# A two-layer decoder trunk on one core: first stage and turn of layers reordered, squares of x moved from GpSimd to ScalarE

## The chip, the core and the metric

The kernel runs on one core of a Trainium2 chip. The metric is the device time of one execution in microseconds (us). Of the kernel before three runs are shown, with a median of 2258.12 us (2257.59 to 2258.47); one more execution was taken with the profiler. Engines are TensorE (PE; its weight loads PEld), VectorE (DVE), ScalarE (ACT), GpSimd (POOL) and SyncE (SP), which here only issues loads and stores.

## The reference

One sequence of 256 tokens with 2048 features passes two layers (DEPTH is 2), all in float32:

```python
for i in range(DEPTH):
    u = rms_norm(h, norm_mix_g[i]) @ w_in[i]
    y_pool = multiscale_pool(u[..., :o1], pool_w[i], pool_scale[i])
    y_att = latent_attention(u[..., o1:o2], u[..., o2:o3], u[..., o3:], cos, sin, ...)
    h = h + jnp.concatenate([y_pool, y_att], axis=-1) @ w_out[i]
    h = h + conv_gated_ffn(rms_norm(h, norm_ffn_g[i]), w_up[i], conv_w[i], conv_b[i], w_down[i])
    gate = jax.nn.sigmoid(rms_norm(h, norm_ple_g[i]) @ w_ple_gate[i])
    h = h + (p[i] @ w_ple[i]) * gate
return rms_norm(h, final_norm_g)
```

rms_norm divides each token's features by the root of their mean square and multiplies by a gain. The inner width of the FFN is 5632, the latents have 512 features each, and cos and sin are rotary tables from the positions.

## The kernel before

**Arithmetic.** Each product of float32 matrices is made of three matmuls on a split (`three`, L1417 to L1421): both operands are cut in a rounded part `hi` and a rest `lo`, and hi x hi, lo x hi and hi x lo are added in PSUM. So each weight passes ScalarE (a copy to `w_hi`, L618 or L837) and VectorE (`w_lo = raw - w_hi`, L1016) ahead of TensorE.

**Weights.** All weights stream in chunks of 1 MB (2048 columns by 128 partitions) through four slots of `raw`, issued by SyncE (`load`, L347). A chunk is split in two halves of 1024 columns, into six slots of `w_hi` and `w_lo`. ScalarE and VectorE work AHEAD = 4 halves ahead: `steps(l, a, b)` makes the splits of halves a+4 to b+3. The semaphores that order this are raw_landed, hi_done, lo_done and w_used.

**Activations.** h holds the residual, tokens on partitions. `turn_h` transposes 256 of its columns on TensorE (four transposes, L1476) into one bank of PSUM; `gained` copies the bank to `hi` on ScalarE with the norm's gain as scale (L637) and the rest to `lo` on VectorE (L1027). One such piece is a "job"; the eight jobs of the first norm are `mix_job(l, 0..7)`. The norm's per-token factor comes later: it is applied when the product is read from PSUM (`latent`, L685), so the mean square is needed only there. GpSimd turns sums of squares into that factor (`factor`).

**First stage.** SyncE issues the rows of the gains (four loads), the conv taps and bias (three loads), and then the chunks of w_in. ScalarE issues the positions and blocks 0 and 1 of x, GpSimd blocks 2 and 3 (a block is 512 columns of h, 512 KB). TensorE transposes the rows of the gains, which VectorE copies to `prm` (L1003) once its 18 set-up steps of the rotary angles (L965 to L999) are done; then it makes turns 0 to 3, transposes taps and bias (L1492), and enters the loop over layers. The first product (block "cq") has eight halves; turns 4, 5 and 6, 7 follow its second and fourth half. ScalarE takes sine and cosine (L628, L629, each function with its table load), jobs 0 and 1, splits 0 and 1, jobs 2 and 3, and in the loop splits 2 to 5, jobs 4 and 5, the squares of block 3 of x, splits 6 and 7, jobs 6 and 7. GpSimd builds the bands of the pooling, and then squares blocks 0 to 2 of x (`sq_x`, L523) and adds them up in nine halving steps (L528).

**Turn of the layers.** In the last stage of a layer (the gate of the per-layer input, four blocks) each block of h becomes final in `gate(j)` on VectorE. ScalarE squares blocks 0 to 2 between the splits there, and block 3 in the next layer, or behind the loop after the last. The halves of the last block are followed by turns 0 to 3 of the next layer, jobs 0 to 3, splits 0 and 1 of the next layer, and then `gate_tanh(3)` and `gate(3)`. These run in the last layer too, where nothing uses them. At the end GpSimd makes the last factor, VectorE scales h (L1402), and SyncE stores it.

Of the kernel before, what the change touches and what calls it, by code (L numbers as in the profile page):

```python
# [114 lines left out]
def build(nc, x, p, positions, norm_mix_g, w_in, pool_w, pool_scale, q_norm_g, w_uq, kv_norm_g, w_ukv,  # L115
# [37 lines left out]
    with ExitStack() as ctx:  # L153
# [3 lines left out]
        def sem(name):  # L157
            return ctx.enter_context(nc.semaphore(name))


        raw = sb("raw", [P, RAW_SLOTS, CHUNK])
# [11 lines left out]
        band_lo = sb("band_lo", [P, len(POOL_WINDOWS), 16], F32R)  # L173
# [5 lines left out]
        krt = (sb("krt_hi", [P, 2, S], F32R), sb("krt_lo", [P, 2, S], F32R))  # L179
        sumsq = sb("sumsq", [P, TT, N_BLK])  # L180
        sumsq_lat = sb("sumsq_lat", [P, 2, TT])
        rstd = {n: sb(f"rstd_{n}", [P, TT]) for n in ("mix", "q", "kv", "ffn", "ple", "final")}
# [4 lines left out]
        mx = sb("mx", [P, 2, TT])  # L187
        nmx = sb("nmx", [P, 2, TT])
        psums = sb("psums", [P, 2, TT])
        prec = sb("prec", [P, 2, TT])  # L190


        with ExitStack() as scope:
# [11 lines left out]
            sq_x = sb("sq_x", [P, TT, N_BLK - 1, BLK], scope=scope)  # L205
# [38 lines left out]
        raw_landed = [sem(f"raw_landed{i}") for i in range(RAW_SLOTS)]  # L244
        slot_seen = sem("slot_seen")
# [22 lines left out]
        x_sq = sem("x_sq")  # L268
# [37 lines left out]
        HJ = KT // 2  # L306

# [28 lines left out]
        def _(sp):  # L336
# [30 lines left out]
            sp.dma_start(rows_g[POOL_S:POOL_S + PKT], pool_scale.rearrange("l (k p) -> k l p", p=P)).then_inc(  # L367
                rows_landed, 16)


# [6 lines left out]
            with sp.Fori(0, L) as l:  # L377
                c = CH["cq"]
                for k in range(KT // 4):
                    load(l, c, square(w_in, l, k, D_POOL))  # L380
                    c += 1
# [65 lines left out]

            for c in range(AHEAD // 2):
# [11 lines left out]
        def _(pool):  # L460
# [23 lines left out]
            for j in range(2, N_BLK):  # L484
                load_x(pool, j)
# [1374 lines left out]
```

## Time and profile before

| | us |
|---|---|
| median of three runs | 2258.12 |
| the profiled execution | 2256.0 |
| its span, first to last instruction | 2254.4 |
| TensorE busy | 2217.3 (98%) |
| VectorE busy | 1387.4 (62%) |
| ScalarE busy | 1046.5 (46%) |
| GpSimd busy | 66.5 (3%) |

The profiled execution is 1.6 us longer than its span and 2.1 us below the median. "Busy" is the time in which an engine has an instruction under way; matmuls overlap, so one of 0.39 us may follow the one before by less. The granted clock is TensorE's, as a share of full speed. An entry such as "PE acc L1419 <- DVE w_lo L1016: 6.1, 2, 5.1" reads: TensorE waited for VectorE's w_lo, 6.1 us in total, 2 times, at most 5.1 us.

### The profile page before, as it was taken

The page shows a single profiled execution, that of the slowest core. Times are in us where ns is not written, and L with a number is a line of the kernel's source. Part 1 is how long each engine was busy: PE and PEld are TensorE (multiplying, and loading weights), DVE is VectorE, ACT ScalarE, POOL GpSimd, SP SyncE. Part 2 cuts the span into 40 slices and gives each one's busy share as a digit, 9 for nine tenths or more (in the row PEclk, how much of TensorE's full clock was granted, in tenths as well). Part 3 has the DMA queues.
Part 4 walks back from the last instruction along what each step waited for, and adds up shares of the span by engine and source line. Part 5 has one row for each costly group of instructions (what it writes and reads, how often), then busy time and mean ns, then how long its engine had stood idle before and what let it go on. Part 6 is the DMA issues. An engine that isn't in the chain of part 4 may idle for free.

```text
span 2254.4 us, 31518 instructions
## 1 busy us (share of the span) xinstructions
PE 2217.3 (98%) x10594; PEld 1856.8 (82%) x10594; DVE 1387.4 (62%) x1768; ACT 1046.5 (46%) x1353; POOL 66.5 (3%) x152
## 2 busy tenths in 40 slices
PE   6999999999999999999999999999999999999997
PEld 5898888888888888888888988888888888888885
DVE  6567566565666565666466665566656566666755
ACT  4545544444444444446454554444444444444553
POOL 7000000000000000000000000000000000000000
PEclk9999999999999999999999999999999999999998
DMA  6653555556555555555556355555555655555562
GB/s 202 206 167 130 203 177 186 186 177 196 186 186 186 186 174 199 186 172 196 173 179 186 132 169 187 180 197 176 190 179 171 201 198 175 189 180 170 188 217 75
DMA packets 233597, 406.60 MB, mean 180 GB/s; under 512 B 14937, under 2 KB 50217, under 8 KB 233385
## 3 DMA queue, kind: packets, MB, share of 16 engines
q1 hardware_dynamic: 232041, 401.87, 53.8%
q0 software_dynamic: 656, 2.63, 0.3%
q10 hardware_dynamic: 816, 1.05, 0.2%
q8 instruction: 44, 0.72, 0.1%
q14 instruction: 40, 0.33, 0.0%
HBM read 403.42 MB, written 2.10 MB: 180 GB/s over the span
## 4 chain that ended last, share of the span: by engine, by line
PE 97%; DVE 1%; issue 1%; DMA 0%; ACT 0%; SPq 0%; DVEq 0%; ACTq 0%; POOLq 0%; POOL 0%
PE acc L1419 31%; PE acc L1421 31%; PE acc L1420 31%; PE tps L1476 3%; PE tps L1420 0%; PE tps L1421 0%; DMA raw<-in_w_in 0%; PE tps L1419 0%; DVE w_lo L1016 0%; PE tps L1669 0%; DVE h L1402 0%; ACT w_hi L618 0%; DVE xa_lo L1027 0%; DVE sg L1369 0%; DVE h L1374 0%
## 5 line engine op out<-in xcount | busy, mean ns | idle before, releaser
L1016 DVE TENSOR_TENSOR w_lo<-raw,w_hi 128x1024 fp32r<-128x1024 f32 (+1 forms) x770 | 919.2, 1224 | 506.8 <-ACT w_hi L837 355.2
L837 ACT ACTIVATE w_hi<-raw 128x1024 fp32r<-128x1024 f32 x508 | 525.9, 1059 | 512.2 <-PE acc L1421 512.2
L1419 PE MATMUL acc<-w_hi,xa_hi 128*128 128x512 f32 (+1 forms) x1792 | 690.5, 385 | 10.9 <-DVE w_lo L1016 6.1
L1421 PE MATMUL acc<-w_lo,xa_hi 128*128 128x512 f32 (+1 forms) x1792 | 687.1, 383 | 0.0
L1420 PE MATMUL acc<-w_hi,xa_lo 128*128 128x512 f32 (+1 forms) x1792 | 686.7, 383 | 0.0
L1419 PEld LDWEIGHTS acc<-w_hi,xa_hi 128*128 128x128 f32 x1792 | 337.5, 188 | 75.8 <-issue 10.4
L1421 PEld LDWEIGHTS acc<-w_lo,xa_hi 128*128 128x128 f32 x1792 | 337.1, 188 | 65.5
L1420 PEld LDWEIGHTS acc<-w_hi,xa_lo 128*128 128x128 f32 x1792 | 337.5, 188 | 64.2
L618 ACT ACTIVATE w_hi<-raw 128x1024 fp32r<-128x1024 f32 (+1 forms) x262 | 263.9, 1043 | 159.7 <-PE acc L1421 150.3
L1419 PE MATMUL acc<-w_hi,gt_hi 128*128 128x512 f32 x640 | 254.7, 398 | 0.0
L1420 PE MATMUL acc<-w_hi,gt_lo 128*128 128x512 f32 x640 | 253.1, 395 | 0.0
L1421 PE MATMUL acc<-w_lo,gt_hi 128*128 128x512 f32 x640 | 253.1, 395 | 0.0
L1419 PE MATMUL acc<-w_hi,xb_hi 128*128 128x512 f32 x560 | 220.7, 394 | 0.0
L1421 PE MATMUL acc<-w_lo,xb_hi 128*128 128x512 f32 x560 | 218.2, 390 | 0.0
L1420 PE MATMUL acc<-w_hi,xb_lo 128*128 128x512 f32 x560 | 218.1, 389 | 0.0
L1234 DVE TENSOR_TENSOR h<-acc,h 128x512 f32<-128x512 f32 x192 | 123.3, 684 | 89.9 <-PE acc L1421 89.9
L1421 PEld LDWEIGHTS acc<-w_lo,gt_hi 128*128 128x128 f32 x640 | 120.3, 188 | 28.9
L1420 PEld LDWEIGHTS acc<-w_hi,gt_lo 128*128 128x128 f32 x640 | 120.4, 188 | 28.0
L1419 PEld LDWEIGHTS acc<-w_hi,gt_hi 128*128 128x128 f32 x640 | 120.4, 188 | 27.9
L1421 PEld LDWEIGHTS acc<-w_lo,xb_hi 128*128 128x128 f32 x560 | 105.1, 188 | 22.2
L1419 PEld LDWEIGHTS acc<-w_hi,xb_hi 128*128 128x128 f32 x560 | 105.2, 188 | 21.3 <-DVE w_lo L1016 0.4
L1420 PEld LDWEIGHTS acc<-w_hi,xb_lo 128*128 128x128 f32 x560 | 105.2, 188 | 20.9
(204 smaller groups left out, 1365.4 us busy)
## 6 DMA issues: line engine op xcount, KB each, us to landing
raw<-in_w_up SPq DMA_DIRECT2D x176, 1024.0 KB, 5.1
raw<-in_w_down SPq DMA_DIRECT2D x88, 1024.0 KB, 5.0
raw<-in_w_out SPq DMA_DIRECT2D x32, 1024.0 KB, 5.1
raw<-in_w_ple_gate SPq DMA_DIRECT2D x32, 1024.0 KB, 5.1
raw<-in_w_in SPq DMA_DIRECT2D x24, 1024.0 KB, 5.4
raw<-in_w_ukv SPq DMA_DIRECT2D x8, 1024.0 KB, 5.8
raw<-in_w_in SPq DMA_DIRECT2D x8, 864.0 KB, 4.8
raw<-in_w_uq SPq DMA_DIRECT2D x6, 1024.0 KB, 5.9
```

The costliest lines, as they stand in the source:

```text
L618: copy(w_hi[:, half_of(m), 0:n], raw[:, c % RAW_SLOTS, at:at + n], ACT.Copy).then_inc(hi_done, 1)
L837: copy(w_hi[:, half_of(m), :], raw[:, c % RAW_SLOTS, (m % 2) * HALF:(m % 2 + 1) * HALF], ACT.Copy).then_inc(hi_done, 1)
L1016: dve.tensor_tensor(w_lo[:, half_of(m), 0:n], raw[:, c % RAW_SLOTS, at:at + n], w_hi[:, half_of(m), 0:n].bitcast(F32), ALU.subtract).then_ ...
L1234: dve.tensor_tensor(hb, acc[b % 2][:, t, :], hb, ALU.add).then_inc(acc_free[b % 2], 1)
L1419: pe.matmul(dst, a_hi, b_hi, start=first, stop=False)
L1420: pe.matmul(dst, a_lo, b_hi, start=False, stop=False)
L1421: return pe.matmul(dst, a_hi, b_lo, start=False, stop=last)
L1476: ins = pe.transpose(bank[:, i * S + t * P:i * S + (t + 1) * P], tiles(t, i), ident[:, :])
```

## The change

- Loads: the first chunk of w of each layer is loaded in two transfers of half the size, the first with a semaphore of its own (`load_first`). ScalarE's queue issues block 0 of x, then the gains' rows, then blocks 1 to 3 of x. SyncE's queue issues the positions, taps and bias, then w. GpSimd's queue has no x.
- Squares: `sq_x` and its sums are gone from GpSimd. ScalarE squares all four blocks of x in the first stage, and of h in the same place of the next layer, or all four behind the loop after the last layer.
- Order: four halves instead of two are split before the loop and before each turn of layers (split 0 ahead of jobs 0 and 1, split 1 behind them, splits 2 and 3 behind jobs 2 and 3); sine, cosine and their table loads move between split 1 and job 2. VectorE copies the first gains in the middle of the angle steps. Taps and bias are transposed between turns 1 and 2. TensorE waits for one job per half instead of for two jobs per two halves.
- Buffers: small tiles are merged or declared first, so that the large buffers start at multiples of 512 bytes.

```diff
+            def load_first(l):
+                sp.wait_ge(lo_done, 2 * CHUNKS * l + 2)
+                sp.sem_inc(slot_seen, 1)
+                for i, landed in enumerate((first_landed, raw_landed[0])):
+                    sp.dma_start(raw[:, 0, i * HALF:(i + 1) * HALF].rearrange("p (a b) -> p a b", b=BLK),
+                                 rows(w_in, l, 2 * i, 2, D_POOL, BLK)).then_inc(landed, 16)
...
-            for i, g in enumerate((norm_mix_g, norm_ffn_g, norm_ple_g)):
-                sp.dma_start(rows_g[KT * i:KT * (i + 1)], g.rearrange("l (k p) -> k l p", p=P)).then_inc(
-                    rows_landed, 16)
...
+                sp.dma_start(pos_i[:, :], positions.rearrange("o (t p) -> p (o t)", p=P)).then_inc(pos_landed, 16)
...
-            for j in range(2, N_BLK):
-                load_x(pool, j)
...
-            for j in range(N_BLK - 1):
-                pool.wait_ge(x_landed[j], 16)
-                hb = h[:, :, j * BLK:(j + 1) * BLK]
-                pool.tensor_tensor(sq_x[:, :, j, :], hb, hb, ALU.mult).then_inc(x_sq, 1)
-            steps, width = N_BLK - 1, BLK // 2
-            while width:
...
             load_x(act, 0)
-            load_x(act, 1)
+            for i, g in enumerate((norm_mix_g, norm_ffn_g, norm_ple_g)):
+                act.dma_start(rows_g[KT * i:KT * (i + 1)], g.rearrange("l (k p) -> k l p", p=P)).then_inc(
+                    rows_landed, 16)
+            act.dma_start(rows_g[POOL_S:POOL_S + PKT], pool_scale.rearrange("l (k p) -> k l p", p=P)).then_inc(
+                rows_landed, 16)
+            for j in range(1, N_BLK):
+                load_x(act, j)
...
+            split(0, 0)
             act.wait_ge(prm_ready, 1)
             mix_job(0, 0)
             mix_job(0, 1)
-            split(0, 0)
             split(0, 1)
+            act.wait_ge(dve_setup, DVE_REDUCED)
+            copy(sin[:, :, :], red[:, 0], ACT.Sin).then_inc(act_setup, 1)
+            copy(cos[:, :, :], red[:, 1], ACT.Sin).then_inc(act_setup, 1)
+            copy(table_word[:, :], inv_freq[:, 0:1], ACT.Tanh)
             mix_job(0, 2)
             mix_job(0, 3)
+            split(0, 2)
+            split(0, 3)
...
+                def x_squares(j):
+                    act.wait_ge(x_landed[j], 16)
+                    squares(l, j, j - N_BLK + 1)
+                steps(l, 0, 2)
                 for i in range(4, 6):
                     mix_job(l, i)
-                squares(l, N_BLK - 1, 0)
+                x_squares(0)
                 steps(l, 2, 4)
                 for i in range(6, 8):
                     mix_job(l, i)
-                steps(l, 4, 8)
+                x_squares(1)
+                steps(l, 4, 5)
+                x_squares(2)
+                steps(l, 5, 6)
+                x_squares(3)
+                steps(l, 6, 8)
...
-                squares(l, 2, 2 * N_BLK + 3)
+                steps(l, e0 + 30, e0 + 34)
                 act.wait_ge(prm_ready, l + 3)
                 for i in range(4):
                     mix_job(l + 1, i)
-                steps(l, e0 + 32, e0 + 34)
+                steps(l, e0 + 34, e0 + 36)
                 gate_tanh(3)
-            squares(L, N_BLK - 1, 0)
+            for j in range(N_BLK):
+                squares(L, j, j - N_BLK + 1)
...
+            def first_gains():
+                dve.wait_ge(prm_t, 1)
+                dve.tensor_copy(prm[:, 0:ROWS_G], acc[1][:, 0, 0:ROWS_G]).then_inc(prm_ready, 1)
...
+            first_gains()
             magic = 1.5 * 2.0 ** 23
...
-                    jobs_split(l, JB["mix"] + 2 * i + 1)
-                    square_halves(l, m, b, xa, 2 * i, 2 * i + 2)
+                    for k in (2 * i, 2 * i + 1):
+                        jobs_split(l, JB["mix"] + k)
+                        square_halves(l, m, b, xa, k, k + 1)
```

## Rows read from the trace of the kernel before

**Rows 1.** Page: busy time and instructions; the costliest line (count, busy us, mean ns).
```profile
PE 2217.3 (98%) x10594; PEld 1856.8 (82%) x10594; DVE 1387.4 (62%) x1768; ACT 1046.5 (46%) x1353; POOL 66.5 (3%) x152
...
L1016 DVE TENSOR_TENSOR w_lo<-raw,w_hi 128x1024 fp32r<-128x1024 f32 (+1 forms) x770 | 919.2, 1224 | 506.8 <-ACT w_hi L837 355.2
```

**Rows 2.** TensorE's waits, whole run: total us, times, longest us.
```profile
PE acc L1419 <- DVE w_lo L1016: 6.1, 2, 5.1
PE acc L1419 <- DVE xa_lo L1027: 4.7, 1, 4.7
PE tps L1476 <- ACT up_tok L856: 2.9, 2, 1.4
```

**Rows 3.** Windows: us, busy of PE, PEld, DVE, ACT, POOL, clock, DMA share, GB/s.
```profile
3.00:7.00 4.00, 0.00 (x0) 0.00 (x0) 3.56 (x15) 0.82 (x1) 4.00 (x21) 1.00 0.96 243
...
17.40:20.20 2.80, 2.75 (x7) 2.17 (x8) 2.80 (x5) 0.97 (x3) 2.73 (x5) 1.00 1.05 387
...
36.50:40.70 4.20, 4.20 (x10) 3.33 (x11) 4.20 (x6) 0.00 (x0) 3.93 (x4) 0.50 0.39 132
```

**Rows 4.** Timeline to the first matmul: start us, us, engine, operation [idle before].
```profile
4.30 53.32 SPq L347 DMA_DIRECT2D raw<-in_w_in  x12
...
14.92 2.00 ACT L618 ACTIVATE w_hi<-raw 128x1024 fp32r<-128x1024 f32 x2 [3.41 <-DMA raw<-in_w_in]
...
17.45 0.79 PE L1419 MATMUL acc<-w_hi,xa_hi 128*128 128x512 f32 x1 [5.12 <-DVE w_lo L1016]
```

**Rows 5.** VectorE in the first stage; then ns (shortest/median/longest) of L1016 and L523.
```profile
22.82 11.97 DVE L1016 TENSOR_TENSOR w_lo<-raw,w_hi 128x1024 fp32r<-128x1024 f32 x4 [1.28 <-ACT w_hi L618]
...
L1016 DVE TENSOR_TENSOR w_lo<-raw,w_hi x2: 2911/2912/2914, 24.7 to 27.5; 128x1024 fp32r<-128x1024 f32 x2
...
L523 POOL TENSOR_TENSOR sq_x<-h x3: 1893/2869/2876, 21.8 to 26.4; 128x1024 f32<-128x1024 f32 x3
```

**Rows 6.** ScalarE's table load; ScalarE's queue, 3 to 7 us; x's landing; angle steps.
```profile
8.55 1.28 ACT L631 ACT_TABLE_LOAD   x1
9.85 0.20 ACT L631 ACTIVATE table_word<-inv_freq 128x1 f32<-128x1 f32 x1
...
q10 hardware_dynamic: 483, 0.95, 93.5%
...
DMA to landing us min/median/max: 4.7/7.1/8.7
...
4.41 0.23 DVE L984 TENSOR_SCALAR turns<-turns 128x128 f32<-128x128 f32 x1
...
6.57 1.53 DVE L999 TENSOR_SCALAR red<-red 128x128 f32<-128x128 f32 x1
```

**Rows 7.** Timeline: the factor's end, normalised rows on VectorE; TensorE's turns of them (chain).
```profile
44.92 0.73 POOL L547 TENSOR_TENSOR rstd_mix<-mean,consts 128x2 f32<-128x2 f32 x1
...
54.19 0.88 DVE L1071 TENSOR_SCALAR lat<-lat,rstd_q 128x512 f32<-128x512 f32 x2
...
59.15 0.95 PE tps L1476 x8
```

**Rows 8.** Timeline at the turn of the layers: ScalarE and TensorE.
```profile
1135.74 3.90 ACT L618 ACTIVATE w_hi<-raw 128x1024 fp32r<-128x1024 f32 x4 [2.63 <-issue]
...
1139.14 0.50 PE L1419 MATMUL acc<-w_hi,xa_hi 128*128 128x512 f32 x1 [1.01 <-DVE w_lo L1016]
```

**Rows 9.** Chain of the last matmuls (first and last of 13); timeline of the last squares.
```profile
2235.92 0.23 PE acc L1421
...
2238.64 0.24 PE acc L1421
...
2242.73 0.63 ACT L657 ACTIVATE sq_h<-h 128x512 bf16<-128x512 f32 x1 [2.56 <-DVE h L1374]
```

**Rows 10.** TensorE's lines by form: count, busy us, mean ns, idle before.
```profile
L1420 PE MATMUL acc<-w_hi,xa_lo 128*128 128x512 f32 x1664 | 649.0, 390 | 0.0
...
L1420 PE MATMUL acc<-w_hi,gt_lo 128*128 128x512 f32 x640 | 253.1, 395 | 0.0
```

More of the change, by code:

```diff
@@ L158, in sem @@
             return ctx.enter_context(nc.semaphore(name))
+        sumsq = sb("sumsq", [P, TT, N_BLK])
+        sumsq_lat = sb("sumsq_lat", [P, 2, TT])
+        rstds = sb("rstds", [P, 6, TT])
+        rstd = {n: rstds[:, i, :] for i, n in enumerate(("mix", "q", "kv", "ffn", "ple", "final"))}
+        band_lo = sb("band_lo", [P, len(POOL_WINDOWS), 16], F32R)
         raw = sb("raw", [P, RAW_SLOTS, CHUNK])
@@ L186, in build @@
         C_D, C_LORA, C_EPS, C_POWER, C_HALF = range(5)
[L187 to L190, printed above, removed]
+        soft = sb("soft", [P, 4, 2, TT])
+        mx, nmx, psums, prec = (soft[:, i] for i in range(4))
         with ExitStack() as scope:
@@ L378, in _ @@
                 c = CH["cq"]
-                for k in range(KT // 4):
-                    load(l, c, square(w_in, l, k, D_POOL))
-                    c += 1
+                load_first(l)
+                for k in range(1, KT // 4):
+                    load(l, c + k, square(w_in, l, k, D_POOL))
+                c += KT // 4
                 for col in (D_POOL + LORA, D_POOL + LORA + LW):
@@ L928, in _ @@
                 gate_tanh(0)
[L929 to L931 removed]
+                steps(l, e0 + 12, e0 + 20)
                 gate_tanh(1)
                 pw_out(1)
[L934 removed]
                 steps(l, e0 + 20, e0 + 30)
                 gate_tanh(2)
[L937 to L938 removed]
+                steps(l, e0 + 30, e0 + 34)
                 act.wait_ge(prm_ready, l + 3)
@@ L1037, in mix_job @@
                 gained(l, JB["mix"] + i, xa, 2 * i, G_MIX + 2 * i, hT_hi, 3 * HJ * l + i + 1)
+            split(0, 0)
             mix_job(0, 0)
             mix_job(0, 1)
-            split(0, 0)
             split(0, 1)
@@ L1044, in _ @@
             mix_job(0, 3)
+            split(0, 2)
+            split(0, 3)
             dve.wait_ge(prm_t, 2)
@@ L1059, in _ @@
                 dve.wait_ge(prm_ready, l + 2)
-                steps(l, -2, 2)
+                steps(l, 0, 2)
                 for i in range(4, 6):
@@ L1382, in _ @@
                 gate(2)
-                steps(l, e0 + 30, e0 + 32)
+                steps(l, e0 + 30, e0 + 34)
                 dve.tensor_copy(prm, prm_all[:, bass.ds(l + 1, 1), :].rearrange("p a b -> p (a b)")).then_inc(
@@ L1391, in _ @@
                     mix_job(l + 1, i)
-                steps(l, e0 + 32, e0 + 34)
+                steps(l, e0 + 34, e0 + 36)
                 gate(3)
@@ L1487, in _ @@
                 turn_h(0, JB["mix"], i)
-            pe.wait_ge(conv_landed, 16 * 3)
-            pe.wait_ge(prm_ready, 1)
-            for l in range(L):
-                pe.transpose(acc[1][:, l, TAP[0]:TAP[2]], rows_c[0][:, l, :], ident[0:2 * FKT, 0:2 * FKT])
-                ins = pe.transpose(acc[1][:, l, TAP[2]:G_Q], rows_c[1][:, l, :], ident[0:2 * FKT, 0:2 * FKT])
-            ins.then_inc(prm_t, 1)
+                if i == 1:
+                    pe.wait_ge(conv_landed, 16 * 3)
+                    pe.wait_ge(prm_ready, 1)
+                    for l in range(L):
+                        pe.transpose(acc[1][:, l, TAP[0]:TAP[2]], rows_c[0][:, l, :], ident[0:2 * FKT, 0:2 * FKT])
+                        ins = pe.transpose(acc[1][:, l, TAP[2]:G_Q], rows_c[1][:, l, :],
+                                           ident[0:2 * FKT, 0:2 * FKT])
+                    ins.then_inc(prm_t, 1)
             with pe.Fori(0, L) as l:
```

56 lines of the change are left out of this document (17 added, 39 removed).

## The prediction

> **What bounds the kernel now.** I read the busy times first. TensorE is busy 2217.3 of 2254.4 us, so neither a faster copy nor a faster load in the middle of a layer can show; only TensorE's 37 us of idleness and its slow stretches can [rows 1]. The view of waits, taken for TensorE alone, says where it stands inside the run: 5.1 us for the first split of w, 4.7 us for a split of x, 1.0 us for another split of w, and twice 1.4 us for up_tok, which the change does not touch [rows 2]. To this come the start before any operand has landed and 15.5 us of tail (2254.4 less 2238.88, the end of the last matmul) [rows 9]. So the case is decided in the first 50 us, at the turn of the layers, and in the tail.
>
> The windows of the first stage then show a second loss. From 36.5 to 40.7 us, right behind the wait of 4.7 us, the granted clock is 0.50 (1.2 GHz): 10 matmuls took 4.2 us [rows 3]. At full clock one follows the other by 0.227 us (2238.64 less 2235.92, over 12, in the chain of waits) [rows 9]; 10 of them are 2.3 us, so the slow clock costs 1.9 us. The first matmuls run at the low pace too: 7 in the 2.75 us from 17.45, where 12 would have fitted [rows 3, 4].
>
> **The squares of x leave GpSimd: the largest term.** Behind the wait of 4.7 us stands VectorE: four subtractions of w_lo took 11.97 us in the very stretch in which GpSimd squares x [rows 5]. Two of them lasted 2.91 us each and GpSimd's squares 2.87 us; the mean of all 770 is 1.22 us [rows 1, 5]. VectorE is held while GpSimd works on x. The Trainium skill (SBUF — State Buffer, "SBUF: two separate sides") says that the pair of ports which these two engines share is an exclusive lock, taken also by a VectorE operation with two SBUF inputs against a GpSimd operation that reads SBUF. By that rule, the trace agrees: durations equal in pairs.
>
> With the squares on ScalarE these subtractions cost 1.23 us. The four give back 7 us of VectorE time and the wait of 4.75 us (31.74 to 36.49) goes whole, with its slow clock of 1.9 us: together **6.7 us**. What is late next? I laid out the eight halves of the first block with 1.05 us per copy of w, 0.78 us per pair of gained copies, 1.23 us per subtraction, 0.83 us per pair of gained subtractions, 1.27 us per block of squares. TensorE needs 12 x 0.227 = 2.72 us a half and 1.05 us for each group of eight turns. ScalarE does 8 copies, 4 pairs and 4 squares from the loop's head, 16.6 us in the 25 us that TensorE takes. With the start below (first matmul at 14.7) the third half is ready 2.3 us ahead of TensorE, the fifth 2.0 us, the seventh 2.5 us: no stall. The fifth is the tightest because ScalarE waits there for VectorE's copies of the gains (1.3 us), which follow the fourth half.
>
> The skill's price for a table switch speaks against this. The trace first: a load took 1.28 us, and the next activation began 0.02 us after it [rows 6]. Two such loads and three small activations, 3.3 us, now stand on ScalarE between the second split and the third x job. The skill (ScalarE: Activation LUTs, "What ACT_TABLE_LOAD costs") gives about 2.66 us a switch, with a drain. By that figure ScalarE would be 2.8 us later, and the third and fifth halves would stall 0.9 us in all. I go by the row.
>
> The mean square is later, relative to the block: the fourth square ends as TensorE finishes the block, and GpSimd's factor takes some 2.2 us more, five small operations of which the last is 0.73 us [rows 7]. So ScalarE reads the block 0 to 1.5 us later than the 0.3 us of before. The cover is there: the normalised rows were ready at 55.07 and TensorE turned them at 59.15, 4.1 us of slack [rows 7]. Cost 0.
>
> **The start.** Before, the 1 MB chunk was issued at 4.30 and landed by 14.92, and the first matmul came at 17.45 [rows 4]. Three things decide now.
> - Loads. While x was on ScalarE's queue it had 93.5% of the busy time, with rows waiting on SP's, at 243 GB/s; later w alone ran at 387 GB/s [rows 3, 6]. [...] The first block of x landed 4.7 us after issue, the median block 7.1 [rows 6]; issued at 0.93 it lands at 5.6. Behind it come 0.24 MB of small rows (0.8 us) and half a chunk (0.52 MB at 387: 1.35 us). With a transfer ending some 1.1 us ahead of its landing, the half lands at about 8. The second block had landed by 9.7 at the latest (8.07, when TensorE's turns began, and two groups of 0.8 us each); with the rows and one or two halves between, 2.2 to 3.5 us, less 0.5 for the earlier issue, it comes at 10 to 12.5. If instead all of x goes first (2.1 MB at 243 are 8.6 us) the half lands at 14.
> - VectorE. The copy of the first gains moves ahead of the last eight steps of the angles, and these ran 4.41 to 8.10, 3.7 us [rows 6]. They now wait for the gains' rows, which lie behind x's first block: landed at about 8, transposed and copied 0.7 us later at 8.75, steps until 12.4 (11.2 if the last, 1.53 us beside GpSimd's memset, is short). Then split 1.35 us, x job 0.83 us, 0.15 us to TensorE: first matmul at **14.7**.
> - Issues. ScalarE's queue now issues four loads of x and four of rows, 0.5 and 0.4 us each: until 4.6, then its first table load of 1.28, before anything has landed. Positions stay first, on SP's queue, which carries the taps next. GpSimd is rid of two issues, and its bands are done sooner. The taps' transposes move between the second and third turn and wait for gains (8.75) and taps, under VectorE's steps.
> - TensorE. Its own order asks for the second block of x and eight turns (1.7 us) before the loop: 11.7 to 14.2. Hidden.
>
> That is 2.75 us gained. Bounds: 13.0 (VectorE's steps short, gains early) and 17.5 (all x first), a gain of 0 to 4.5 us. I take 2.75, from the row of VectorE's steps, which hold even if the load is 2 us late. The six slow matmuls at the start remain. The block ends at 14.7 + 21.8 + 1.2 + 2.1 = 39.8 us against 49.5.
>
> **The turn of the layers.** Behind its last gate_tanh ScalarE lost 2.63 us, with nothing that it waited for, before it began the next layer's splits at 1135.74, and TensorE stood 1.01 us before 1139.14 for them [rows 8]. Now these two halves are split ahead of gate_tanh and the loop's edge, behind the first two, in what was ScalarE's idle time before the first turns of the new layer (that is the move of steps e0+32 to e0+34). Fifth and sixth halves, needed 5 us later, cover the edge. The squares of three blocks leave the layer's end and join the next layer's first 24 us. **1.0 us** gained; at least 0, at most 1.0.
>
> **The tail.** After the last matmul: gate_tanh, gate, squares of block 3, three operations on GpSimd, eight on VectorE. All four squares now come after gate_tanh. ScalarE idled 2.56 us before 2242.73 [rows 9], so it is free at 2240.17; four blocks of 2 x 0.63 us end at 2245.3, where one ended at 2244.1. Loss **1.3 us** (rounded up by GpSimd's steps). If leaving the loop costs ScalarE what its repetition did (2.63 us), it is 3.8 us. I take 1.3: the program runs on straight there.
>
> **Nothing.** One more issue of some 0.4 us per layer for the half loads: at the second layer no wait for a landing is among TensorE's [rows 2]. The merged tiles and the new semaphores put no instruction on TensorE's path. The 512-byte starts: TensorE's pace shows no mark of where its operands lie, 0.390 and 0.395 us for the second product with xa_lo and gt_lo, which lie in different buffers [rows 10]. From 1 ns lost to 1 ns won on 8,688 such matmuls would be 9 us either way, so this zero is the widest of the bounds; I keep it as a rival.
>
> **Sum.** -2.75 - 6.65 - 1.0 + 1.3 = -9.1 us. The profiled execution took 2256.0 us (1.6 around the span of 2254.4), now 2246.9; the median of 2258.12 goes to **2249.0**.
>
> **Rivals.**
> - *All x first.* x on one queue keeps the SP queue out, as between 3 and 7 us. First matmul at 17.5, gain 6.35: 2251.8. Against: that share was measured with two transfers of x and only tiny ones beside them.
> - *ScalarE becomes the bound.* Two table loads, four squares and a fixed order: if the fifth half is late by 5 us, TensorE stalls 3 and pays 1.9 for the clock: 2253.9. For: only 2.0 us of slack, on steps estimated one by one. Against: the rest of the first stage has 2 us to spare at each half.
> - *GpSimd was not the cause.* If the subtractions stay at 2.9 us, the 6.65 us stay: 2255.6. Against it the pairs of equal durations.
> - *Slower: the addresses.* All large buffers move by some hundred bytes. Place: each matmul that reads them. Price: 1 ns each is 8.7 us, and from 1.05 ns on (9.1 over 8,688) the kernel is not faster; at 2 ns it takes 2266. For it speaks only that the same matmul's second product has 0.390 and 0.395.
> - *The tail's edge*: 3.8 for 1.3: 2251.5.
>
> **Chances.** Forecast 0.62 (its own range 2246 to 2251), all x first 0.13, tail's edge 0.08, ScalarE 0.07, GpSimd not the cause 0.05, addresses 0.05, a third of that a gain. This kernel can be told from no change at 0.2%, 4.5 us: below 2253.6 is faster. The first three are, with a third of ScalarE's case and the addresses' gain: 0.87. Within 0.2%: 0.10, the rest of ScalarE's case and GpSimd's. Slower: 0.03, the addresses. Range 2245.0 to 2253.8: below, the earliest start (1.75 more) and a tail that costs nothing; above, ScalarE's case.
>
> **What would show it.** Right: w_lo at 1.2 to 1.4 us throughout the first 40 us; no wait over 2 us on TensorE after its first matmul; clock 1.00 from 20 us on; ScalarE's reading of the first block at about 40; no wait at 1130 us; squares from 2240.2 to 2245.3 and an end 15 to 17 us after the last matmul. Wrong: a first matmul after 16, w's first half behind all of x; a wait for ScalarE before the third or fifth half; a first square later than 2241; a pace other than 0.227 us.

## The result, and the profile after

The changed kernel takes **2231.93 us** (median of 4 runs, 2231.72 to 2233.44); the kernel before took 2257.86 us beside it (median of 4, 2256.82 to 2258.47). The ratio is 0.9887, with a 95% interval of 0.987 to 0.9904: 25.9 us faster, where 9.1 were forecast, and below the range of the prediction. The profiled execution took 2233.44 us around a span of 2231.8, so the two profiled spans differ by 22.6 us. The medians differ by 3.3 us more, because the profiled execution of before lies 1.9 us under its median and that of after 1.5 us above. The sums below are made on the spans.

Busy times and TensorE's waits of the changed kernel (TensorE's lines stand eight lines lower in the code: L1419 to L1421 are now L1427 to L1429; the subtraction of w_lo, L1016, is L1023):

```profile
PE 2203.0 (99%) x10594; PEld 1855.2 (83%) x10594; DVE 1383.2 (62%) x1770; ACT 1053.6 (47%) x1368; POOL 47.3 (2%) x138
...
L1023 DVE TENSOR_TENSOR w_lo<-raw,w_hi 128x1024 fp32r<-128x1024 f32 (+1 forms) x772 | 914.5, 1214 | 506.8 <-ACT w_hi L844 352.1
```

```profile
PE acc L1422 <- DMA rows_g<-in_pool_scale: 6.7, 1, 6.7
PE tps L1484 <- ACT up_tok L863: 2.9, 2, 1.4
PE tps L1484 <- DMA h<-in_x: 2.0, 1, 2.0
PE acc L1427 <- DVE xa_lo L1034: 0.8, 1, 0.8
```

Of the waits of [rows 2], the 6.1 us for w_lo are gone (5.1 at the start, 1.0 at the turn of the layers) and the 4.7 us for xa_lo in the first stage as well; what is left of them is 2.8 us ahead of the first matmul. But look at the first line against [rows 1]: TensorE executes the same 10594 instructions and is busy **14.3 us less**. A kernel that only lost waits would be busy as long as before. The slow clock of [rows 3] did not return, which is 1.9 us of it; against that, 12 matmuls instead of 6 run at the low pace at the start (below), about 1.2 us more. The rest needs another source.

Timeline of the start (start us, us, engine, operation, idle before), then of the rest of the first block:

```profile
3.12 1.02 SPq L353 DMA_DIRECT2D raw<-in_w_in  x2
...
7.22 0.22 DVE L978 COPY prm_all<-acc 128x56 f32<-128x56 f32 x1 [0.55 <-PE acc L1422]
...
9.78 0.24 DVE L1008 TENSOR_SCALAR red<-red 128x128 f32<-128x128 f32 x1
...
10.98 1.06 ACT L615 ACTIVATE w_hi<-raw 128x1024 fp32r<-128x1024 f32 x1 [4.28 <-DMA raw<-in_w_in]
...
11.59 1.97 PE L1484 MATMUL tps<-ident,h 128*128 128x128 f32 x8 [1.99 <-DMA h<-in_x]
...
12.13 1.23 DVE L1023 TENSOR_TENSOR w_lo<-raw,w_hi 128x1024 fp32r<-128x1024 f32 x1 [2.10 <-ACT w_hi L615]
...
14.37 0.79 PE L1427 MATMUL acc<-w_hi,xa_hi 128*128 128x512 f32 x1 [0.81 <-DVE xa_lo L1034]
```

```profile
25.12 2.36 DVE L1023 TENSOR_TENSOR w_lo<-raw,w_hi 128x1024 fp32r<-128x1024 f32 x2 [1.29 <-ACT w_hi L615]
...
39.40 1.43 POOL L536 TENSOR_TENSOR rstds<-mean,consts 128x2 f32<-128x2 f32 x1
...
40.53 0.29 PE L1427 MATMUL acc<-w_hi,xa_hi 128*128 128x288 f32 x1
...
40.86 1.27 ACT L692 ACTIVATE lat<-acc,rstds 128x512 f32<-128x512 f32 x2 [1.87 <-POOL rstds L536]
```

The first matmul comes at 14.37 us (before 17.45, [rows 4]), and TensorE leaves the first block at 40.53 (before 49.47). The first 12 matmuls, up to 19.65 us, start 0.43 us apart; in the kernel before it was 6, up to 20.17. (The column of the clock reads 1.00 there in both kernels, so the low pace at the start is seen in the starts alone.) Later the windows show what was won: in 36.5 to 40.7 us, where ten matmuls ran at half clock in [rows 3], 21 run at full clock.

```profile
17.40:20.20 2.80, 2.80 (x9) 2.14 (x9) 1.57 (x4) 2.79 (x8) 2.72 (x5) 1.00 1.05 409
...
36.50:40.70 4.20, 4.20 (x21) 3.50 (x20) 2.76 (x3) 2.49 (x6) 2.85 (x5) 1.00 0.50 120
```

At the turn of the layers ScalarE still loses its 3 us at the loop's edge, [3.18 <-issue], but TensorE waits nowhere near it. In the tail the squares follow gate_tanh at once, and from the last matmul's end to the end of the span are 16.27 us (before 15.52).

```profile
1120.75 2.01 ACT L615 ACTIVATE w_hi<-raw 128x1024 fp32r<-128x1024 f32 x2 [3.18 <-issue]
```

```profile
2216.79 0.63 ACT L656 ACTIVATE sq_h<-h 128x512 bf16<-128x512 f32 x1
...
2223.29 5.39 DVE L1410 SCALAR_TENSOR_TENSOR h<-h,rstds,fin_g 128x512 f32<-128x512 f32 x8 [3.87 <-POOL rstds L587]
2224.73 4.35 SPq L459 DMA_DIRECT2D out<-h  x4
```

First block 8.9 us less, turn 1.0 less, tail 0.75 more: 9.2 us. Of the 22.6, **13.4 are still missing**, and none of them is a wait. (The 3.3 us between medians and spans fit the start too. The first block ended at 51.67 and 51.72 us in two later profiles with the order of before, and at 38.94 and 39.08 in two with the order of after, so the profiled pair understates what the start gained in most executions.)

They lie in the middle of the layers. TensorE's lines by form (count, busy us, mean ns, idle before), first before, then after:

```profile
L1419 PE MATMUL acc<-w_hi,gt_hi 128*128 128x512 f32 x640 | 254.7, 398 | 0.0
...
L1421 PE MATMUL acc<-w_lo,gt_hi 128*128 128x512 f32 x640 | 253.1, 395 | 0.0
```

```profile
L1428 PE MATMUL acc<-w_hi,xa_lo 128*128 128x512 f32 x1664 | 648.4, 390 | 0.0
...
L1427 PE MATMUL acc<-w_hi,gt_hi 128*128 128x512 f32 x640 | 250.7, 392 | 0.0
...
L1428 PE MATMUL acc<-w_hi,gt_lo 128*128 128x512 f32 x640 | 249.1, 389 | 0.0
```

The products with xa and xb are as they were. All three with gt are about 6 ns shorter, 640 of each; the three with ppt, 32 of each, go from 396 to 390 too. A mean duration is no pace, since matmuls overlap, so the pace is read from the starts. One follows the other as in these two stretches of TensorE's timeline, 12 matmuls apart, of before and of after:

```profile
372.98 0.40 PE L1419 MATMUL acc<-w_hi,gt_hi 128*128 128x512 f32 x1
...
375.78 0.40 PE L1419 MATMUL acc<-w_hi,gt_hi 128*128 128x512 f32 x1
```

```profile
363.91 0.39 PE L1427 MATMUL acc<-w_hi,gt_hi 128*128 128x512 f32 x1
...
366.63 0.39 PE L1427 MATMUL acc<-w_hi,gt_hi 128*128 128x512 f32 x1
```

Before, 2.80 us over 12 are 0.2333 us each; after, 2.72 over 12 are 0.2267. With 3 x 640 + 3 x 32 = 2016 such matmuls, 6.7 ns less each are 13.4 us. Added up over the whole trace instead of two stretches, the time from the start of each of these 2016 matmuls to the next start is 12.8 us less, so nearly all of the missing part is here and 0.6 us of it is not accounted for. No instruction of these stages was changed. What did change is where their tiles start: before, raw, w_hi and w_lo, xa and xb started at 128 bytes past a multiple of 512, gt and ppt at 192; now all start at a multiple of 512. (The starts are added up from the sizes of the tiles in the code; no view shows an address.)

### The profile page after: what moved, and what is told of

Same layout as the page of the kernel before. It is cut to its first block, busy times and chain, and to the rows that moved or that the text cites. A ratio compares the mean times of both kernels' runs of the same rounds, so it can differ in the third digit from the quotient of the medians.

```text
span 2231.8 us, 31546 instructions
## 1 busy us (share of the span) xinstructions
PE 2203.0 (99%) x10594; PEld 1855.2 (83%) x10594; DVE 1383.2 (62%) x1770; ACT 1053.6 (47%) x1368; POOL 47.3 (2%) x138
## 4 chain that ended last, share of the span: by engine, by line
PE 98%; ACT 0%; DVE 0%; DMA 0%; issue 0%; SPq 0%; ACTq 0%; POOLq 0%; DVEq 0%; POOL 0%
PE acc L1427 31%; PE acc L1429 31%; PE acc L1428 31%; PE tps L1484 3%; PE tps L1428 1%; PE tps L1429 0%; PE tps L1427 0%; DMA raw<-in_w_in 0%; PE tps L1679 0%; DVE h L1410 0%; DVE w_lo L1023 0%; ACT sq_h L656 0%; ACT w_hi L615 0%; ACT up_tok L863 0%; PE tps L1574 0%
## 5 line engine op out<-in xcount | busy, mean ns | idle before, releaser
L1023 DVE TENSOR_TENSOR w_lo<-raw,w_hi 128x1024 fp32r<-128x1024 f32 (+1 forms) x772 | 914.5, 1214 | 506.8 <-ACT w_hi L844 352.1
L1427 PE MATMUL acc<-w_hi,xa_hi 128*128 128x512 f32 (+1 forms) x1792 | 690.4, 385 | 0.8 <-DVE xa_lo L1034 0.8
L1429 PE MATMUL acc<-w_lo,xa_hi 128*128 128x512 f32 (+1 forms) x1792 | 686.8, 383 | 0.0
L1429 PEld LDWEIGHTS acc<-w_lo,xa_hi 128*128 128x128 f32 x1792 | 336.9, 188 | 65.8
L1427 PEld LDWEIGHTS acc<-w_hi,xa_hi 128*128 128x128 f32 x1792 | 337.2, 188 | 65.2 <-issue 1.6
L1427 PE MATMUL acc<-w_hi,gt_hi 128*128 128x512 f32 x640 | 250.7, 392 | 0.0
L1429 PE MATMUL acc<-w_lo,gt_hi 128*128 128x512 f32 x640 | 249.1, 389 | 0.0
L1427 PE MATMUL acc<-w_hi,xb_hi 128*128 128x512 f32 x560 | 220.7, 394 | 0.0
L1429 PE MATMUL acc<-w_lo,xb_hi 128*128 128x512 f32 x560 | 218.2, 390 | 0.0
L1429 PEld LDWEIGHTS acc<-w_lo,gt_hi 128*128 128x128 f32 x640 | 120.1, 188 | 25.0
L1427 PEld LDWEIGHTS acc<-w_hi,gt_hi 128*128 128x128 f32 x640 | 120.2, 188 | 24.2
L1429 PEld LDWEIGHTS acc<-w_lo,xb_hi 128*128 128x128 f32 x560 | 105.1, 188 | 22.1
L1427 PEld LDWEIGHTS acc<-w_hi,xb_hi 128*128 128x128 f32 x560 | 105.2, 188 | 21.1 <-DVE w_lo L1023 0.4
```

The source lines that it names most:

```text
L1023: dve.tensor_tensor(w_lo[:, half_of(m), 0:n], raw[:, c % RAW_SLOTS, at:at + n], w_hi[:, half_of(m), 0:n].bitcast(F32), ALU.subtract).then_ ...
L1427: pe.matmul(dst, a_hi, b_hi, start=first, stop=False)
L1429: return pe.matmul(dst, a_hi, b_lo, start=False, stop=last)
```

## The experiments

All were timed against the kernel before on the same chip, four runs each or more. Starts are given in bytes past a multiple of 512. In `three` the left operand of a product is a piece of xa, xb, gt or ppt, 128x128, which is loaded into the array; the right one is w_hi or w_lo, of which 512 columns stream past it. The views print the two in the other order (`w_hi,gt_hi`).

**Are the addresses the missing part?** First the whole change with the old starts.

```
+        pad_a = sb("pad_a", [P, 32])      # ahead of raw
+        pad_b = sb("pad_b", [P, 16])      # ahead of gt, ppt
```

> The whole change, except that two pads put the large buffers back at 128 and the buffers of the FFN (gt, ppt, gate_tok) back at 192 bytes beyond a multiple of 512, as before. Theory A (TensorE reads a left operand more slowly when it starts at 64 beyond a multiple of 128; the rest of the change did what the prediction's sum says): about 9 us faster than before (-8.9 first block, -1.0 turn, +0.8 tail), and the products with gt follow one another by 0.233 us as before. Theory B (the addresses do nothing; the missing 13 us come from the order of loads and splits): 23 to 26 us faster, as the changed kernel.

It took 2245.46 us (2245.02 to 2245.77), ratio 0.9947 (0.993 to 0.9963). The products with gt went back to 398, 395 and 395 ns. So the reordering is worth 12.7 us (2258.12 beside it) and the addresses 13.5. Then the other half of the same question: the kernel before with 64 bytes more ahead of gt (e2), which puts gt and ppt at 256, with w left at 128.

```
+        pad = sb("pad", [P, 16])          # in the kernel before, ahead of gt, ppt
```

> The kernel before with one pad of 64 bytes ahead of the buffers of the FFN and the attention, which puts them at 256 beyond a multiple of 512; nothing else. Theory A with 128 bytes as the step: 13.4 us faster (1920 products with gt and 96 with ppt, 6.7 ns each), median about 2244.5. If it needs 512 bytes: no change. Theory B: no change.

It took 2254.26 us (2253.24 to 2255.85; ten runs), ratio 0.9984 (0.9975 to 0.9994). The products with gt stayed at 397, 395 and 394 ns, so the 13.4 us did not come. My theory, that the left operand wants a start at a multiple of 128 or 256, fell. This kernel did gain 3.9 us, though its profiled span, 2254.2, shows 0.2. The trace has a part of it: gt's matmuls start 232.4 ns apart on average, where in the kernel before it is 233.3, 1.7 us in all, and the profiled execution, the slowest of the ten, lost that again in the first block, which ended at 51.67 us (49.47 in the profile of before). The rest is open.

**Which operand, and by how much?** Three kernels move left operands away from the changed kernel's starts, with w left at 0: xa to 64 (by its pads xb, gt and ppt came to 128), gt alone to 64, gt alone to 32 (ppt, behind it, came to 128 in both).

```
+        pad_a = sb("pad_a", [P, 16])      # xa64: ahead of xa (and pad_b ahead of xb)
...
+            pad_g = sb("pad_g", [P, 16], scope=scope)   # gt64: ahead of gt (pad_h ahead of ppt)
```

> The changed kernel with xa (the left operand of most products) at 64 beyond a multiple of 512 and all behind it at 128. Theory A: each of 5376 products with xa takes 6.7 ns more, +33 to +36 us against the changed kernel, so some 8 to 10 us slower than before (about 2267). Theory A': the address matters only for gt's place in memory: no change against the changed kernel (2232). Theory B: no change.

> The changed kernel with gt_hi and gt_lo alone at 64 beyond a multiple of 512 (what lies behind them at 128). Theory A: 1920 products take 6.7 ns more, 12.8 us slower than the changed kernel, about 2244.8; weight loads unchanged in length. Theory B: 2232.

> As the one before, with gt at 32 beyond a multiple of 512. If the cost is one more piece of memory touched by a row of 512 bytes that does not start at a multiple of 128, it costs the same 12.8 us; if it grows as the start is less aligned, up to twice that; if only 64 is bad, 0.

xa64 took 2284.02 us, ratio 1.0119 (1.0102 to 1.0136): slower than the kernel before. gt64 took 2244.92 and gt32 2244.79, 13.0 and 12.9 us above the changed kernel. In the trace of gt64 only the products of the moved tiles, gt and ppt, are longer, and by the same 6 ns; 32 bytes cost as much as 64.

```profile
L1430 PE MATMUL acc<-w_hi,xa_lo 128*128 128x512 f32 x1664 | 648.0, 389 | 0.0
L1429 PE MATMUL acc<-w_hi,gt_hi 128*128 128x512 f32 x640 | 254.3, 397 | 0.0
L1431 PE MATMUL acc<-w_lo,gt_hi 128*128 128x512 f32 x640 | 252.6, 395 | 0.0
```

xa64 missed its number because xb and gt, at 128, were slow as well (395 and 394 ns in the second product), though 128 was where xa and xb had been fast in the kernel before. What differs is w: at 128 there, at 0 here. That is the thought that settled the case: not the place of an operand counts but **the distance between the two**.

**The right operand, and everything together.** If the distance counts, moving w away from the rest must slow all 8688 products of 512 columns, and moving all tiles by the same 64 bytes must cost nothing.

```
+        pad_a = sb("pad_a", [P, 16])      # w64: ahead of w_hi (pad_b: the rest at 128)
...
+        pad_a = sb("pad_a", [P, 16])      # all64: ahead of raw
```

> The changed kernel with w_hi and w_lo, the right (moving) operands of nearly all products, at 64 beyond a multiple of 512. If only the left operand's start matters: 2232, no change. If the right one's matters as much: 8700 products by 6.7 ns, 58 us slower.

> The changed kernel with one pad of 64 bytes ahead of raw: every large buffer, left operands and right ones, starts at 64 beyond a multiple of 512. The runs so far: products are slow (395 to 396 ns) wherever the left operand and w differ in their place within 512 bytes (gt 64 or 32 with w at 0; gt at 256 with w at 128; xa at 64, xb at 128 with w at 0; w at 64 with xa at 128) and fast (390) where they agree (all at 0; xa and w at 128). Theory D (only the difference counts): all products at 390 ns, 2232. Theory E (an absolute place counts: 0 is good and 64 is bad): 8700 products slower by some 6.2 ns, about 2286.

w64 took 2285.64 us, 53.7 above the changed kernel: 6.2 ns on each of 8688. Products of other shapes did not follow: in w64 those of 288 columns keep their 295 ns, and those of 256 columns, in which w is the operand that is loaded, are 4 ns shorter (281 for 285).

```profile
L1429 PE MATMUL acc<-xb_hi,w_hi 128*128 128x256 f32 x160 | 44.9, 281 | 0.2
L1431 PE MATMUL acc<-w_lo,xa_hi 128*128 128x288 f32 x128 | 37.8, 295 | 0.0
```

all64 took 2232.96 (2231.89 to 2234.11), ratio 0.9895 (0.9878 to 0.9911). Its products with gt are at 392, 389 and 389 ns, 64 bytes off every multiple of 128; the 1.0 us above the changed kernel is within the spread of its runs. Now the distance alone is taken from the kernel before, with no tile at 512: its six small tiles of factors merged and 64 bytes added, which put gt and ppt at 128, like w.

```
-        rstd = {n: sb(f"rstd_{n}", [P, TT]) for n in ("mix", "q", "kv", "ffn", "ple", "final")}
+        rstds = sb("rstds", [P, 6, TT])
+        rstd = {n: rstds[:, i, :] for i, n in enumerate(("mix", "q", "kv", "ffn", "ple", "final"))}
...
+        pad = sb("pad", [P, 16])
```

> The kernel before with six small tiles merged into one and a pad of 64 bytes, so that gt and ppt stand at 128 beyond a multiple of 512 like w, xa and xb. No buffer that TensorE reads in its long products starts at a multiple of 512. Theory D: gt's products fall from 396 to 390 ns, 13.4 us faster, about 2244.5. Theory E' (512-byte starts are needed): no change, 2258.

It took 2244.62 us (2243.89 to 2245.33) beside 2257.78, ratio 0.9944 (0.9927 to 0.996): 13.2 us from the distance alone, with the order of before and, in its profile, waits of much the same size (11.6 us for w_lo and xa_lo, 10.8 in [rows 2]).

```profile
L1421 PE MATMUL acc<-w_hi,gt_hi 128*128 128x512 f32 x640 | 250.7, 392 | 0.0
L1423 PE MATMUL acc<-w_lo,gt_hi 128*128 128x512 f32 x640 | 249.1, 389 | 0.0
L1422 PE MATMUL acc<-w_hi,gt_lo 128*128 128x512 f32 x640 | 249.1, 389 | 0.0
```

**The period, and one right operand of two.** gt and ppt 256 bytes away from w; then w_lo alone 64 bytes away from all others, which stand at 256.

```
+            pad_g = sb("pad_g", [P, 64], scope=scope)   # gt256
...
+        pad_a = sb("pad_a", [P, 16])      # wlo64: ahead of w_lo; band_lo and a pad_b bring the rest back
```

> The changed kernel with gt and ppt at 256 beyond a multiple of 512, w at 0. If any difference within 512 bytes costs: 2016 products 6.2 to 6.7 ns slower, +13 us, 2245. If the period is 256 bytes: 2232.

> The changed kernel with w_lo alone 64 bytes off: all other large buffers are at 256 beyond a multiple of 512, w_lo at 320. If each product pays by its own pair (or by w_lo being read while the next left operand is loaded), about a third of 8700 products pay: +18 us, 2250. If one buffer off slows all: +54, 2286.

gt256 took 2231.98 us (392, 389, 389 ns), so 256 bytes apart is as good as 0. With e2 (128 apart: slow) the list is: 0 and 256 cost nothing; 32 and 64 cost 6.6 ns from start to start, averaged over all of gt's matmuls; 128 costs a little less, 5.6 ns in e2 and 5.9 in xa64. A period of 256 bytes fits all of them; 192 apart was not tried. wlo64 took 2273.93 us, 42 above the changed kernel. Neither a third of the cost (18 us, only the products with w_lo) nor all of it (54) was right, and its lines show why the simple picture fails: all three products are slow, those with w_hi too, at 394 to 397 ns.

```profile
L1429 PE MATMUL acc<-w_hi,xa_hi 128*128 128x512 f32 x1664 | 660.0, 397 | 0.1
L1431 PE MATMUL acc<-w_lo,xa_hi 128*128 128x512 f32 x1664 | 655.8, 394 | 0.0
L1430 PE MATMUL acc<-w_hi,xa_lo 128*128 128x512 f32 x1664 | 655.7, 394 | 0.0
```

w_lo streams in one product of three only, and the loaded operands all stand where w_hi does, so two products of three touch no tile that is off. Yet from each start to the next it is 231.3 to 232.7 ns on average, whichever two of the three kinds follow each other. So a rule that looks at one product's own two operands does not describe this kernel; which pair it is that counts stays open, and w_hi alone was not tried.

| starts: w, xa, xb, gt | slow products | median us | above the changed kernel |
|---|---|---|---|
| before: 128, 128, 128, 192 | gt, ppt (2016) | 2257.86 | 25.9 |
| order of before: 128, 128, 128, 256 (e2) | gt, ppt | 2254.26 | 22.3 |
| order of before: 128, 128, 128, 128 | none | 2244.62 | 12.7 |
| after: 0, 0, 0, 0 | none | 2231.93 | 0 |
| order of after, starts of before | gt, ppt | 2245.46 | 13.5 |
| gt64; gt32 (ppt at 128) | gt, ppt | 2244.92; 2244.79 | 13.0; 12.9 |
| all64: 64, 64, 64, 64 | none | 2232.96 | 1.0 |
| gt256: 0, 0, 0, 256 | none | 2231.98 | 0.05 |
| xa64: 0, 64, 128, 128 | all (8688) | 2284.02 | 52.1 |
| w64: 64, 128, 128, 128 | all | 2285.64 | 53.7 |
| wlo64: w_lo 64 away from all | all three kinds | 2273.93 | 42.0 |

**The terms of my own sum, one by one.** First the largest: GpSimd's squares taken out of the kernel before.

```
-            for j in range(N_BLK - 1):
-                ...
-                pool.tensor_tensor(sq_x[:, :, j, :], hb, hb, ALU.mult).then_inc(x_sq, 1)
-            ...
+            pool.memset(sumsq[:, :, 0:N_BLK - 1], 512.0).then_inc(x_sq, 1)
```

> The kernel before with GpSimd's squares of blocks 0 to 2 of x and their nine sums left out (it writes a constant in their place, so the first layer's mean square is not computed from x). Theory (GpSimd held VectorE): the subtractions of w_lo between 22 and 35 us take 1.2 us instead of 2.9, the wait of 4.7 us and the stretch at clock 0.50 are gone, 6.65 us faster, about 2251.3. Rival (the subtractions were slow for another reason): they stay at 2.9 us, no change.

It took 2251.78 us (2249.81 to 2252.31) beside 2258.12, ratio 0.9972 (0.9961 to 0.9984): 6.3 us, where the term was 6.65. In its profile the first matmul came 1.7 us later than in that of before (19.15 for 17.45), and the stretch from there to the end of the block took 26.5 us for 32.0. The wait for xa_lo is gone from TensorE's waits, the two for w_lo are still there, and four subtractions take 4.63 us where they took 11.97 in [rows 5]:

```profile
PE acc L1409 <- DVE w_lo L1006: 6.0, 2, 5.1
PE tps L1466 <- ACT up_tok L846: 2.9, 2, 1.4
```

```profile
25.39 4.63 DVE L1006 TENSOR_TENSOR w_lo<-raw,w_hi 128x1024 fp32r<-128x1024 f32 x4 [1.29 <-ACT w_hi L608]
```

Then the start: the gains' copy behind all the steps of the angles again, the first chunk in one load again, and the changed kernel once more beside it.

```
-            first_gains()                  # gains_late: the same call behind the last step
...
+                sp.dma_start(raw[:, 0, :].rearrange("p (a b) -> p a b", b=BLK),   # one_load
+                             rows(w_in, l, 0, 4, D_POOL, BLK)).then_inc(raw_landed[0], 16)
```

> The changed kernel with VectorE's copy of the first gains behind all 18 steps of the angles again, as before. In the changed kernel the copy is at 7.22 and the steps end at 10.02, then VectorE is idle until 12.13. My prediction held that moving the copy forward cost time, since the steps then wait for the gains. With the copy late the steps start at about 6.7 and end at 9.5, the copy follows; ScalarE's first x job comes only at 11.95. So no change, within 0.5 us. Rival: later gains delay the taps' transposes and turns 2 and 3: up to 1 us slower.

> The changed kernel with the first chunk of w of each layer in one load again. The half landed at 10.95 and 0.52 MB more take 1.35 us at 387 GB/s: first split 1.35 us later, first matmul at 15.7 instead of 14.4, 1.3 us slower (2233.2). Rival: with one transfer of 1 MB ahead of it the second block of x comes later too, up to 1.5 us more in place of the wait for the split, 2233.5. No change would show that the queue's order decides, not the size of the load.

> The changed kernel itself, on the same chip as the three before it: 2231.9, within 0.5 us of its first timing.

gains_late took 2231.75 us (2231.65 to 2232.73), no change: VectorE ends these steps and the copy at 10.13 us, ahead of w's landing at 10.65, and then idles 1.69 us. one_load took 2234.58 (2234.09 to 2235.87) and the changed kernel beside it 2231.97 (2231.64 to 2233.24): 2.6 us for splitting the load, twice what I expected. (The profiled executions of the two differ by 1.4 us only, because that of the changed kernel was the slowest of its four.) In its trace ScalarE begins the first split at 12.33 (10.57 beside it) and the first matmul comes at 15.81 (14.15):

```profile
12.33 1.97 PE L1479 MATMUL tps<-ident,h 128*128 128x128 f32 x8 [2.79 <-DMA h<-in_x]
...
15.81 0.79 PE L1422 MATMUL acc<-w_hi,xa_hi 128*128 128x512 f32 x1 [1.51 <-DVE xa_lo L1029]
```

Block 1 of x landed 1.1 us later as well (12.28 for 11.17). That is not shown to come from the single transfer: in the thirteen profiles with two half loads this block landed anywhere from 10.89 to 12.07. w itself landed at 12.30 with one load, and at 8.50 to 11.21 in the thirteen with two, so the gain for w stands.

The queues in the changed kernel, 9 to 14 us (q1 is SyncE's with w, q10 ScalarE's with x; packets, MB, share), show why w's half takes so long: both move at once, at about half the rate each.

```profile
q1 hardware_dynamic: 500, 0.99, 51.3%
q10 hardware_dynamic: 494, 0.95, 49.1%
```

**A better version?** Two tries on top of the changed kernel. jobs_first puts the first two pieces of x ahead of the first split of w on ScalarE and VectorE, since x is there first. tuned adds to it: squares back at the layer's end, ahead of the tail, and the last scaling shared between VectorE and ScalarE.

```
-            split(0, 0)                    # jobs_first: on ScalarE and VectorE,
+            split(0, 0)                    # now behind x's first two pieces
...
+            for j in range(2):             # tuned: blocks 0 and 1 on ScalarE
+                for t in range(TT):
+                    act.wait_ge(g_fin, TT * j + t + 1)
+                    copy(hb, hb, ACT.Copy, scale=rstd["final"][:, t:t + 1]).then_inc(fin_act, 1)
```

> The changed kernel with x jobs 0 and 1 ahead of split 0 again, on ScalarE and VectorE. In its trace the jobs' turns are done at 9.0 and the gains are there at 7.4, but ScalarE waits for w's first half until 10.98 and the first matmul comes at 14.37. With the jobs first, split 0 ends on VectorE at 13.4: first matmul at 13.5, 0.8 us faster (2231.1). Rival (the second block of x, landed at 11.59, with its turns until 13.6 decides): 0.7 to 0.8, the same within error, so no more than that can come.

> The kernel before this one in the list, and beside it: the squares of blocks 0 to 2 stand where they were before (end of a layer; for x ahead of the loop), and at the end VectorE multiplies blocks 0 and 1 with the final gain while the factor is being made, and ScalarE scales them, beside VectorE's blocks 2 and 3. Tail 16.3 us before: 0.75 less for the squares, 2.65 less for four of VectorE's eight operations. With the 0.8 of the start 4.2 us faster than the changed kernel, 2227.7. Rival (the third square ahead of the loop makes the fifth half late): up to 1.3 us of that is lost.

jobs_first took 2231.89 us (2231.68 to 2232.1), tuned 2231.65 (2231.2 to 2232.03): neither can be told from 2231.93. In the trace of jobs_first the first matmul came at 13.73 us for 14.37, although block 1 of x landed later (12.11 for 11.59). But kernels that start in the order of the changed one have their first matmul anywhere from 12.98 to 14.62, so one profile can't show a gain of 0.8, and the medians show none. In tuned the arithmetic of the tail does shrink. Both engines finish at 2224.8, where VectorE alone finished at 2228.7:

```profile
2222.08 2.56 ACT L970 ACTIVATE h<-h,rstds 128x512 f32<-128x512 f32 x4 [2.10 <-POOL rstds L593]
2222.08 2.74 DVE L1436 SCALAR_TENSOR_TENSOR h<-h,rstds,fin_g 128x512 f32<-128x512 f32 x4 [0.89 <-POOL rstds L593]
2223.44 2.91 SPq L465 DMA_DIRECT2D out<-h  x4
```

But the span ends at 2230.4, 5.6 us after the arithmetic: the four stores, the first of them issued at 2223.44, move 2.10 MB at about 400 GB/s, 5.3 us. In the changed kernel, where the scaling takes longer, the span ends 3.1 us after it. What was gained on the engines was turned into waiting for the output, which I had left out of the sum.

## Why the prediction was right or wrong

- **Failed: the zero of "The 512-byte starts".** The prediction says: "TensorE's pace shows no mark of where its operands lie, 0.390 and 0.395 us for the second product with xa_lo and gt_lo". These two numbers are the mark. In [rows 10] stand the same instruction, the same form and the same right operand, and 5 ns of difference over 640 executions; I read it as noise in a duration and never looked at the starts, where it is 6.7 ns (6.6 on average over all). Two other slips went with it. I priced all 8688 products alike by 1 ns, when only the 2016 of gt and ppt could change. The range left this bound out, though the text called it the widest. And I gave the gain a third of a 0.05 rival, when the rows pointed one way: xa was the fast one, and the change brought all tiles to one start. Both bounds stood there, but their size came from no row. From the rows, 5 ns x 2016 = 10.1 us was the end of that bound, and the forecast would have been 2239, with 2249 at its upper side.
- **Right: GpSimd as the cause of the long subtractions.** Forecast -6.65; -6.3 alone on the kernel before. Subtractions of w_lo (1024 columns) are at 1.2 to 1.4 us all through the first stage, and the stretch at clock 0.50 is gone. The rival that GpSimd was not the cause is out. The Trainium skill (SBUF — State Buffer, "SBUF: two separate sides") calls the pair of ports that VectorE and GpSimd share an exclusive lock. The trace agrees, and so does the experiment: 2.91 us a subtraction beside GpSimd's squares, 1.2 without them.
- **Right in sum by luck: the start.** Forecast first matmul 14.7, measured 14.37. VectorE's steps, by which I set it, ended at 10.02 instead of 12.4 (the gains came at 7.22, not 8.75), and VectorE then idled 2.10 us for ScalarE's split. w's first half landed at 10.96, where I had about 8; block 1 of x at 11.59, within my 10 to 12.5. So the load decides, and that I was 0.3 us off is two errors that cancel. I had worked out the 8 as if x's block, the rows and w's half came one behind the other at full rate, but the two queues moved side by side. Nor does any run show my 1.1 us between a transfer's end and its landing; the last packet of x's block 0 ended at 5.48 us in the trace of before and the block landed at 6.14. The start's other term, "the six slow matmuls at the start remain", was wrong as well: it was 12, and from the first matmul to the end of the block it took 26.2 us where the sum had 25.1. The first block ended at 40.5, against 39.8.
- **Right: no stall of ScalarE in the first stage.** TensorE has no wait after 14.37 us there; the two table loads took 1.28 us each, as in [rows 6], and the next activation began 0.02 us behind each, so the price of a switch that the prediction took from the row holds. The rival "ScalarE becomes the bound" is out, and "all x first" too. ScalarE read the first block 0.03 us after GpSimd's factor was done (40.83), that is the "0 to 1.5 us later" at its lower end.
- **Right: the turn.** 1.0 us gained; the edge of 3.18 us on ScalarE is covered.
- **Nearly: the tail.** +0.75 for +1.3. The squares began at 2216.79, 0.1 us before gate_tanh's last entry ends, so leaving the loop cost ScalarE nothing, and the rival "the tail's edge" is out. The stores behind the scaling take up part of what comes late.

Without the addresses the forecast was 2249.0 and that kernel took 2245.46: 3.5 us better. On the spans of before and after the four terms are 9.2 us of the 9.1 forecast, but this closeness is luck in part: the start gave 3.1 us for 2.75, the rest of the block 5.9 for 6.65, the tail cost 0.75 for 1.3, and by the medians the four terms together are 12.7. The start itself varies between executions: in that kernel's profile the first block ended at 38.84 us, in the changed kernel's two profiles at 40.53 and 40.16, with the same order of work. In the kernel before it moved too: 49.47 us in the profile from which I forecast, 51.67 and 51.72 in two others with its order. That would make up the 3.5 us, but single profiles do not show how often each happens.

## What to carry to other kernels

For long products like these (512 columns of float32 data), start the tiles that TensorE reads as left and right operand at the same place modulo 256 bytes, and look at this first wherever TensorE is busy nearly all the time: it takes a few bytes of padding, it costs no instruction, and no view names it as a wait. It shows as one form of the same matmul a few ns longer than another; when a program's lines by form disagree at equal shape, take the pace from the starts, multiply by the count, and treat that product as a term of the sum, not as a rival. A small difference that does not fit is worth more than a large wait when it stands in a row with thousands of executions.

## What the runs showed of the hardware that was not expected

- Matmuls of 512 columns of float32 data follow each other by 0.2267 us when left and right operand start 0 or 256 bytes apart, by 0.2333 us when the starts are 32 or 64 apart, and by 0.2324 when they are 128 apart (e2). 2016 of them: 12.9 to 13.5 us in four comparisons. All 8688: 53.7. Products of 256 and 288 columns got no longer in w64. The loads of the left operand beside them keep their mean of 0.19 us. Why is not shown; that the load of the next left operand and the streaming of the right one collide is a guess, and w_lo alone, 64 away, costing 42 us and slowing all three products, says that it is not as simple as one load against one stream.
- One transfer of 1 MB for w at the head of its queue, where two of half the size stood, cost 2.6 us (2234.58 against 2231.97). w and x, on two queues, moved at once (0.99 and 0.95 MB in 9 to 14 us), and the landing of the same transfer differed between profiles with the same order of loads: 8.50 to 11.21 us for w's first half.
- In tuned, with nothing else running, 2.10 MB of output in four stores took until 5.6 us after the last arithmetic, 7.0 us after the first store was issued. As long as all four stores stand behind the last factor, scaling that ended 3.9 us sooner shortened the tail by 0.7 us only.
